# An encoder layer with product-key experts: merge units ordered by branch, and a share of weighted sums on TensorE that follows the tile

## What is computed

```
merged = (sigmoid(gate_r) * (y_r @ w_proj_ret)
        + sigmoid(gate_s) * (y_s @ w_proj_sgu)
        + sigmoid(gate_a) * (y_a @ w_proj_att))
h = h + merged @ w_out
h = h + peer_ffn(rms_norm(h), ...)     # per token: 8 heads x 16 experts chosen by two top-16 searches
...
act = gelu(einsum('thkd,td->thk', u_tab[eid], xt))
w = gate * act
out = einsum('thk,thkd->td', w, v_tab[eid])
h = h + sigmoid(rms_norm(h) @ ple_gate) * (p @ ple_proj)
```

## Time and profile before

| | |
|---|---|
| median of 3 runs | 3938.55 us (3936.4 to 3942.12) |
| profiled execution | 3932.46 us, span 3930.7 us |
| PE / DVE / ACT / POOL busy | 79% / 68% / 35% / 31% of the span |
| HBM read, written | 1257.80 MB, 39.85 MB |

### The profile page before, as it was taken

How to read it: one execution, slowest core, us unless ns; L and a number is a source line. 1 busy time by engine, 2 the same in 40 slices (tenths; PEclk the granted TensorE clock), 3 DMA queues, 4 the chain that set the end, 5 groups by cost and what they waited for, 6 DMA issues and landing times. The chain is left out here.

```text
span 3930.7 us, 31118 instructions
## 1 busy us (share of the span) xinstructions
PE 3095.3 (79%) x7816; PEld 1408.4 (36%) x7816; DVE 2684.5 (68%) x5254; ACT 1381.2 (35%) x3577; POOL 1214.4 (31%) x1092
## 2 busy tenths in 40 slices
PE   8979999898789988966888878888766656566556
PEld 4545555543334334422333333333322222222222
DVE  3335555312577777776888787877688888888984
ACT  3223333201344433444443342433444334334332
POOL 0000000000333324443443343444244444443442
PEclk9988998799899999988999888899888789878887
DMA  4330101145999999999999999999999999999995
GB/s 160 120 143 27 41 27 45 64 182 197 381 405 413 409 368 413 409 424 426 414 426 426 426 410 405 419 425 426 367 401 412 427 426 412 427 426 395 426 427 247
DMA packets 213925, 1299.35 MB, mean 331 GB/s; under 512 B 24720, under 2 KB 38288, under 8 KB 69520
## 3 DMA queue, kind: packets, MB, share of 16 engines
q0 software_dynamic: 147456, 1073.81, 65.7%
q1 hardware_dynamic: 60560, 211.34, 14.1%
q10 hardware_dynamic: 5760, 12.59, 0.8%
HBM read 1257.80 MB, written 39.85 MB: 330 GB/s over the span
## 5 line engine op out<-in xcount | busy, mean ns | idle before, releaser
L1311 PE MATMUL l_acc<-l_rows,l_diag 128*128 128x512 f32 x2560 | 1414.0, 695 | 704.9 <-ACT l_diag L1445 696.9
L1213 POOL DMA_INDIRECT l_rows<-in_peer_uv,l_at x1024 | 1197.0, 1169 | 1686.0 <-DVE l_acc L1591 1038.0
L1581 DVE SCALAR_TENSOR_TENSOR l_rows<-l_rows,l_xn 128x1024 f32<-128x1024 f32 x1024 | 1220.3, 1223 | 201.9 <-DMA l_rows<-in_peer_uv,l_at 143.6
L1311 PEld LDWEIGHTS l_acc<-l_rows,l_diag 128*128 128x128 f32 x2560 | 526.2, 217 | 1532.7 <-ACT l_diag L1445 999.0
L1591 DVE SCALAR_TENSOR_TENSOR l_acc<-l_rows,l_wts,l_acc 128x1024 f32<-128x1024 f32 x384 | 493.5, 1285 | 204.8 <-ACT l_wts L1441 204.8
L1437 ACT ACTIVATE l_dots<-l_dots 128x2 f32<-128x2 f32 x512 | 103.6, 202 | 1032.5 <-DVE l_rows L1581 1029.6
L1206 POOL CAST l_at<-l_expert 128x16 uint32<-128x16 f32 x64 | 17.3, 270 | 976.6 <-DVE l_expert L1567 976.4
L117 PE MATMUL l_pa<-all_ring,l_xt 128*128 128x512 f32 x656 | 294.4, 600 | 8.4 <-DMA l_xt<-kept_xnt 8.4
L1441 ACT ACTIVATE l_wts<-l_dots,l_gates 128x1 f32<-128x1 f32 x1024 | 293.5, 287 | 16.8
L117 PE MATMUL l_pa<-l_ring,l_xt 128*128 128x512 f32 x624 | 280.6, 601 | 20.4 <-DMA l_xt<-kept_xnt 13.6
L1445 ACT ACTIVATE l_diag<-all_ident,l_wts 128x128 f32<-128x128 f32 x640 | 257.0, 402 | 21.0
(11 more groups left out here) (243 smaller groups left out, 2824.8 us busy)
## 6 DMA issues: line engine op xcount, KB each, us to landing
l_ring<-in_w_late SPq DMA_DIRECT2D x48, 1024.0 KB, 9.4
all_ring<-in_w_late SPq DMA_DIRECT2D x48, 1024.0 KB, 8.9
l_rows<-in_peer_uv,l_at POOLq DMA_INDIRECT x1024, 16.7
l_yt<-kept_yt SPq DMA_DIRECT2D x48, 256.0 KB, 7.7
kept_s<-l_yt ACTq DMA_DIRECT2D x32, 256.0 KB, 7.5
l_s_in<-kept_s SPq DMA_DIRECT2D x64, 128.0 KB, 6.9
mix_w_branches<-in_w_branches_kept SPq DMA_DIRECT2D x8, 768.0 KB, 4.6
kept_yt<-b_yt SPq DMA_DIRECT2D x8, 768.0 KB, 3.7
```

The source lines that it names most:

```text
L1213: pool.indirect_dma_start(out=rows[:, r % SLOTS, :], out_offset=None, in_=A["peer_uv"], in_offset=bass.IndirectOffsetOnAxis(ap=at[:, c % 2 ...
L1311: ins = pe.matmul(acc2[:, hs], diag[n_pe(r) % DIAGS][:], rows[:, r % SLOTS, D + half * HB:D + (half + 1) * HB], start=first, stop=last)
L1581: dve.scalar_tensor_tensor(out=u, in0=u, scalar=1.0, in1=xn[:, t % 2, :], op0=ALU.mult, op1=ALU.mult, accum_out=dots[:, n:n + 1]).then_inc ...
```

## The change

Three things change, all in the late stage.

1. Units are ordered by branch: unit n takes branch n // 2 and column half n % 2 (before: branch n % 3, half n // 3). The weights are laid out in the same order, so each chunk is still read once per group in file order.
2. A branch output is loaded once per tile and serves both halves: `load_branch` is called for branches 0 and 1 at the start of a group, and for branch 2 when the last `proj` of unit 1 is done. The semaphore counts of `proj` follow.
3. `on_tensor` reads a table by tile: of 8 successive rows, tiles 0 and 1 have 4 on PE, tiles 2 to 4 have 5 (as before), tiles 5 to 7 have 6. Of the 1024 rows, 656 now go to PE and 368 to DVE (before 640 and 384).

```diff
+TENSOR_ROWS = 2 * ((1, 3, 5, 7),) + 3 * ((1, 3, 5, 6, 7),) + 3 * ((1, 2, 3, 5, 6, 7),)
...
 def on_tensor(r):
 
-    return r % 2 == 1 or r % 8 == 6
+    return r % 8 in TENSOR_ROWS[r // NSEL]
...
-        y_of = lambda n, i: yt[:, (n % 2 * K + i) * RW:(n % 2 * K + i + 1) * RW]
+        y_of = lambda br, i: yt[:, (br % 2 * K + i) * RW:(br % 2 * K + i + 1) * RW]
...
-                for n in range(2):
-                    load_branch(g, n)
-
-            def load_branch(g, n):
-
-                if n > 1:
-                    sp.wait_ge(pb_done, plan.of["proj", g, n - 2, len(GROUPS[g]) - 1].pb[0] + 1)
+                for br in range(2):
+                    load_branch(g, br)
+
+            def load_branch(g, br):
+
+                if br == 2:
+                    sp.wait_ge(pb_done, plan.of["proj", g, 1, len(GROUPS[g]) - 1].pb[0] + 1)
                 for i, t in enumerate(GROUPS[g]):
-                    sp.dma_start(y_of(n, i), X["yt"][t][:, n % 3 * RW:(n % 3 + 1) * RW]).then_inc(yt_in[n % 2][i], 16)
+                    sp.dma_start(y_of(br, i), X["yt"][t][:, br * RW:(br + 1) * RW]).then_inc(yt_in[br % 2][i], 16)
...
-                    for n in range(2, UNITS):
-                        if s == plan.of["proj", g, n - 2, len(GROUPS[g]) - 1].slot:
-                            load_branch(g, n)
+                    if s == plan.of["proj", g, 1, len(GROUPS[g]) - 1].slot:
+                        load_branch(g, 2)
...
-                pe.wait_ge(yt_in[job.n % 2][job.i], (nth(job.g, job.i) * 3 - 3 + job.n // 2 + 1) * 16)
-                matmuls(pe, into_pb(job.pb[0])[:], [(y_of(job.n, job.i)[:, c * P:(c + 1) * P], wide_chunk(job.chunk, c)) for c in range(4)]).then_inc(pb_done, 1)
+                br = job.n // 2
+                pe.wait_ge(yt_in[br % 2][job.i], (nth(job.g, job.i) * (2 - br % 2) - (br == 0)) * 16)
+                matmuls(pe, into_pb(job.pb[0])[:], [(y_of(br, job.i)[:, c * P:(c + 1) * P], wide_chunk(job.chunk, c)) for c in range(4)]).then_inc(pb_done, 1)
...
-                half, br = divmod(job.n, 3)
+                br, half = divmod(job.n, 2)
...
     for n in range(UNITS):
-        half, br = divmod(n, 3)
+        br, half = divmod(n, 2)
```

## The result

The changed kernel takes 3904.05 us (median of 4, 3902.92 to 3906.75) against 3940.34 for the kernel before (median of 4): ratio 0.991, 95% interval 0.9893 to 0.9927, so 36 us less. Timed again later, beside three other kernels, it took 3904.34 against 3936.4, ratio 0.9917 (0.9904 to 0.993). The forecast was 3923.5 us, range 3908 to 3938: the direction was right, the gain more than double the 15 us forecast.

A forecast was written before the change was run, and what follows sets the result against it. The prediction took the 16 DMA engines to bound the kernel after about 1000 us. Fewer loads (-12.0 us) and the row split (-3 us), 15 us off the median 3938.55, gave 3923.5 us, range 3908 to 3938.

The forecast's parts named there:

- The reading of the second half: Behind about 1000 us the kernel gathers, and the 16 DMA engines, not a compute engine, are the limit.
- Fewer loads, -12.0 us: Groups 1 and 2: 18 loads of 256 KB leave the full DMA stretch, worth 11.1 to 12.4 us.
- Rival C: PE paces group 1's load slots, so only group 2's 9 loads count: 3932.5 us, or 3938.5 with nothing; chance 0.18.
- Rows between PE and DVE, -3 us: Tiles 0, 1 and 5 to 7: moved rows cost 0 themselves; a quarter of 11.5 us idle DMA returns.
- The bound of 11.5 us: Idle DMA in tiles 0, 1 and 5 to 7 that the row split could give back at most; at least 0.
- The 67 us that PE was to gain in tiles 5 to 7: Tiles 5 to 7: 48 rows moved from DVE add 67 us to PE over some 950 us, beside full DMA.
- Waits on the reordered loads: Branch 2's load, issued after unit 1 and used in unit 4, adds no wait: price 0, 15 us at most uncovered.
- VectorE was to take 41 us more: Tiles 0 and 1: 32 rows moved from PE add 41 us to DVE over some 600 us.
- rival D: Tiles 0 and 1: DVE holds buffers longer, so slower; half of +42 us less 12 gives 3947.5 us; chance 0.10.
- The dip at the group's start: Start of group 1, 1050 to 1100 us: 7.5 us of idle DMA follows the wait for `l_xt` and stays.
- Rival B: The balance was worth more: all 11.5 us idle DMA and small gaps go, 3903.5 to 3915 us; chance 0.12.
- a stretch of group 1 that keeps its length: Failure sign: if the stretch with group 1's merges keeps its length, the change doesn't give back what it removes.

The follow-up runs named there:

- g2: The kernel before with 18 more loads of 256 KB in tile 6, into tiles nothing uses then; 3949.57 us, ratio 1.003.
- e4: The kernel before with 6 of 8 rows on TensorE in tiles 5 to 7 alone; 3937.48 us, ratio 1.0002.
- e1: The changed kernel (units by branch, 24 loads) with the old 5 of 8 rows on TensorE in every tile; 3932.62 us, ratio 0.9988.
- e5: The kernel before with units ordered by branch and nothing else, so 48 loads; 3931.36 us, ratio 0.9988.
- k1: The changed kernel, unaltered, timed and profiled again; 3904.34 us, ratio 0.9917.
- k2: The kernel before (units by half, 48 loads) with the whole new table of rows; 3909.57 us, ratio 0.9931.
- k3: The changed kernel with each branch output loaded twice, so 48 loads; 3909.1 us, ratio 0.9934.
- g1: The kernel before with 18 more loads of 256 KB in tile 0, into tiles nothing uses then; 3934.24 us, ratio 0.9991.
- h3: The changed kernel with 60 overwritten 128x512 matmuls given back to TensorE in group 1's dense products; 3947.51 us, ratio 1.0027.
- e3: The kernel before with 4 of 8 rows on TensorE in tiles 0 and 1 alone; 3913.13 us, ratio 0.9941.

## Why the prediction was wrong

**What bounds the kernel.** The reading of the second half was right only for tiles 5 to 7. There 18 loads cost 12.0 us (g2, interval 7 to 17), which fits the price of 0.67 to 0.69 us a load, and a different split of rows changed nothing by itself (e4). In tiles 0 and 1 it was wrong. "No compute engine is the limit there, the 16 DMA engines are" rested on shares of 0.98 to 1.01 and on two windows from tiles 2 and 5; PE's 47.51 us of 50 stood in the same rows, and 368 to 413 GB/s up to about 1670 us against 426 later in the earlier trace rows.

**Fewer loads, -12.0 us.** The step "18 loads go from the full stretch" failed: with 24 loads (e1) the time was that with 48 (e5), and about 5 us came back once tiles 0 and 1 had 4 of 8 rows on TensorE (k1 against k2 and k3). For the nine loads of group 1 the reason is shown: TensorE set the pace there (g1, h3). For the nine of group 2 it is not. The bytes were right, the queue table moved as forecast. Rival C named this mechanism ("PE paces the slots where group 1's loads go") and I gave it 0.18, since "DMA is at 1.01 in the same window".

**Rows between PE and DVE, -3 us.** This is the step that made the time wrong. I gave the shed work "price 0 by itself" since it lay "beside a full DMA", and allowed only idle DMA to come back, 11.5 us at most. Measured it is 23 us (e3). The shed work itself was read too small by half: "four took 1.88 us" are four records and one row, so 32 rows are 55 to 60 us and not under 30, which the 6.9 us of a gate job with 8 matmuls also says. Had I priced the work in full I would have been wrong to the other side; 23 of 55 us came back. The bound of 11.5 us was none, because idle time of the DMA engines was counted against a full share of 1.01 and not against the full rate: at the 422 GB/s of tile 6 tiles 0 and 1 would be an estimated 21 and 14 us shorter. The 67 us that PE was to gain in tiles 5 to 7 has the same slip; 192 records, not 96, came, and its busy time grew by 65.8 us, since records overlap and count 0.43 us and not their mean of 0.695 each, and since the granted clock rose with the work, from 0.83 to 0.85 in the three tiles to 0.87 to 0.90. That the number fits is luck.

**What was right.** Waits on the reordered loads: none appeared. VectorE was to take 41 us more in tiles 0 and 1 and was busy 37 us longer. POOL's waits for its sums (rival D) grew by 112 us in that stretch, but those for TensorE's fell by 115 and the two tiles got shorter, so D's condition came true and its price didn't. Whether VectorE's work took back part of the gain, no run tells. At 3 of 8 the two tiles are 5 us longer again; whether by this or by VectorE's load no run tells. The dip at the group's start remained: POOL's longest wait there is 23.48 us, after 24.47. Rival B, "the balance was worth more", had the right time at its far end, which the range left out, for a reason that is a part of it at most: from 1400 to 1500 us idle DMA did go, 6.5 us by the shares, but what made the two tiles 20 us shorter was TensorE's work.

**The sign I missed.** The forecast asked tiles 0 to 4 for 12 to 14 us and named as its own failure a stretch of group 1 that keeps its length or tiles 5 to 7 that shrink. It had no sign for tiles 0 and 1 shrinking too much, and that is what came: 20 us.

## What to carry to other kernels

A DMA share near 1 does not say that the DMA engines set the pace: as I read it, gathers waiting in a queue keep it there while a slower lap elsewhere decides when the next is issued. Compare the rate with the best that the same kernel reaches in another stage. Here tiles 0 and 1 lay 4 to 5% below it with TensorE busy 86% and 82% of the time, bytes put into tile 0 cost nothing, and 55 us of work taken off TensorE gave 20 us in the two tiles. So price such work above nothing and below its full duration; the stage can't get shorter than its bytes take at the best rate. Count a kernel's instructions against the profile's records before multiplying by a duration: here one matmul is two records. A few dummy transfers in one stage at a time settle in one run each whether DMA sets its pace.

## What the runs showed of the hardware

The DMA share stays at 0.98 to 0.99 while the rate goes from 395 to 412 GB/s with the number of transfers in the same time, so the share has almost no resolution there. In tile 6, at a share of 1.01, 18 loads of 256 KB took 12.1 us, which is 390 GB/s for them, 8% below the 422 GB/s of the whole tile. A 128x512 float32 matmul shows as two records that start 0.43 us apart at full clock. With 192 records more in tiles 5 to 7 the granted clock was 0.90, 0.87 and 0.88 after 0.83, 0.84 and 0.85.
